# Doubling steps of a blocked RWKV-7 scan on one core: the first two groups issued alternately, the second on the off-diagonal quarters of TensorE's array

## The chip, the cores and the metric

The kernel runs on one core of a Trainium2 chip. The metric is the device time of one execution in microseconds (us), lower is better. The median of three runs before the change is 2687.97 us (2686.44 to 2688.4).

## What is computed

One layer of a diffusion backbone over 512 latent and 128 context tokens of width 1024: input projection, two parallel mixers (a Fourier mixing and a bidirectional RWKV-7 scan), output projection, then an expert-choice FFN with 16 experts. The change touches the scan only. In the reference it is a recurrence over tokens, for 16 heads of 64 channels and both directions:

```python
def wkv7_scan(r, w, k, v, kk, a, s0, reverse):
    def step(S, inp):
        r_t, w_t, k_t, v_t, kk_t, a_t = inp
        sa = jnp.einsum('bhij,bhj->bhi', S, -kk_t)
        S = (S * w_t[:, :, None, :] + sa[..., None] * (kk_t * a_t)[:, :, None, :]
             + v_t[..., None] * k_t[:, :, None, :])
        y = jnp.einsum('bhij,bhj->bhi', S, r_t)
        return S, y
```

## The kernel before, in words

`layer` runs five phases one after the other: `front_phase` (input projection, to about 500 us), `scan_phase` (L434, about 500 to 1316 us), `merge_phase`, `expert_phase` (from about 1600 us, the larger part of the rest) and `combine_phase`. Nothing of a later phase is loaded or computed during the scan.

**The scan.** It makes eight passes (`tiles`, `body(i, m, first, last)`), one for each 128 channels, that is two heads. The tokens lie in five chunks of 128. A chunk, two directions and two heads make four problems, each with a triangular 128x128 system, whose inverse is built by doubling: the diagonal 64x64 quarters are inverted by five rounds on blocks of 64, a sixth round fills in the off-diagonal quarter. A pass has these stages:

- **Pair stage** (`pair_products`, L869 to L893; five chunks in the order `ORDER`). PE forms the products of a chunk: L877 and L878 for the masked matrices, and the 64x64 products into two PSUM banks `b_m(0)`, `b_m(1)` (L886, L888, L892), 20 of them. Row half h of the array, that is partitions `HALVES[h]`, writes bank `b_m(h)`; its outputs go to both column halves. ACT copies them out (L766 to `TD`, L767 to `Mq`, which a trace calls `x`), twice each. POOL then masks: `tt_start` (L647, L649) on `TD` for each chunk, `m_off` (L666) to `Mo`, `t_start` (L654, L658) to `T`. DVE masks `NRR` (L1186). In between, PE, ACT and DVE carry the output norm of the pass before (`norm`).
- **Rounds** (`for rd in range(TOP)`, six). The five chunks are three groups, `GROUPS`: chunks at places 0 and 1, at 2 and 3, and at 4. A group has two PSUM banks, `b_z(b)` and `b_dt(b)`. In a round, for each group: `z_step` makes Z = Mo^T TD (L908; in the sixth round L914) into `b_z`; ACT evicts it to `Z` (L775, `evict`); `t_step` makes T^T Z (L933; sixth round L929) into `b_z` and Z^T T (L939) into `b_dt`; DVE adds the first to `TD` (L1229; in the fifth round L1232, to `TT`), the second to `T` (L1235). POOL writes the next round's `Mo` once the group's `z_step` has read the last (L666). In the sixth round ACT writes `TT` instead (L787). A 64x64 matmul of fp32 is two passes through the array, each with a weight load, and stands as two in the x count. Both halves of the diagonal are used in turn: half 0 (rows and columns 0 to 63) and half 1.
- **Jobs in the rounds.** A round has three places (`PER_ROUND`) in which PE, ACT and DVE carry the next pass's preparation, `front(n, i + 1, 1 - m)`, in this order: J_DEC0, J_DEC1, J_NORM | J_RATE0, J_RATE1, J_VT | J_ST, J_SCAN1, J_SUB1 | J_KEYS1, J_NONE0, J_NONE1 | J_NONE2, J_BONUS. PE's matmul of a job waits until the PSUM of the job before is read (`s_free`). J_DEC0: PE L824, ACT a table load and two sigmoids (L695), a square (L700). J_DEC1: PE L824, ACT L695 again, after which DVE runs the prefix sums (L1086). J_BONUS: DVE L1157. The first pass has no norm, the last pass no jobs of a next pass.
- **Chain** (`part`, `output`): from L967 on, the states chunk by chunk, some 28 us.

**The order of the queues** is written by hand and each engine keeps it. In a round of before:

- PE: z(0), z(1), job 0, t(0) (both products), z(2), job 1, t(1), job 2, t(2). In the sixth round two filler matmuls (`fill(2)`, L945) stand before t(1) and before t(2).
- ACT: evict 0, evict 1, job 0, evict 2, job 1, job 2.
- DVE: for each group in turn: its job, the add to `TD`, the add to `T`.

Of the kernel before, what the change touches and what calls it, by code (L numbers as in the profile page):

```python
# [433 lines left out]
def scan_phase(nc, d, ident, lora, spare):  # L434
# [12 lines left out]
    NG, NPROB = NT, 4  # L447
    ORDER = [0, 3, 1, 2, 4]
    POS = {g: n for n, g in enumerate(ORDER)}
    GROUPS, CHUNKS, BANKS = ((0, 2), (2, 4), (4, 5)), (slice(0, 4, 3), slice(1, 3, 1), slice(4, 5, 1)), ((0, 1), (2, 3), (4, 5))  # L450
    TOP = LEVELS - 1
    steps = [(b, l) for l in range(1, LEVELS) for b in range(len(GROUPS))]
# [17 lines left out]
    with ExitStack() as ctx:  # L470
# [160 lines left out]
        def _(g_):  # L631
# [10 lines left out]
            def body(i, m, first, last):  # L642
# [37 lines left out]
        def _(act):  # L680
# [129 lines left out]
        def _(pe):  # L810
# [57 lines left out]
            def pair_products(i, m, n):  # L868
# [26 lines left out]
            def z_step(i, n):  # L895
                b, l = steps[n]
# [7 lines left out]
                for c, p in enumerate(range(*GROUPS[b])):  # L904
                    if l < TOP:
                        for q in range(NPROB):
                            for hs in HALVES:
                                last = pe.matmul(ps_of(b_z(b), b)[hs, c, q, :], Mo[hs, p, q, :], TD[hs, p, q, :], start=True, stop=True)  # L908
                    else:
                        g = ORDER[p]  # L910
                        for h in range(2):
                            for dr, hs in enumerate(HALVES):
                                os_ = HALVES[1 - dr]
                                last = pe.matmul(ps_of(b_z(b), b, 2)[hs, c, h, :], Mq[os_, g, 2, h, :], TT[os_, g, 2 * dr + h, os_], start=True, stop=True)  # L914
                last.then_inc(s_z, 1)

            def t_step(i, n):
                b, l = steps[n]
                pe.wait_ge(s_zs, i * NS + n + 1)
                if l == 1:  # L920
                    pe.wait_ge(s_ti, i * NGR + b + 1)
                else:
                    pe.wait_ge(s_t, i * ND + n - NGR + 1)
                pe.sem_inc(s_pe_turn, 1)
                for c, p in enumerate(range(*GROUPS[b])):
                    if l == TOP:
                        for h in range(2):
                            for dr, hs in enumerate(HALVES):
                                last = pe.matmul(ps_of(b_z(b), b, 2)[hs, c, h, :], T[hs, p, 2 * dr + h, :], Z[hs, p, h, :], start=True, stop=True)  # L929
                    else:  # L930
                        for q in range(NPROB):
                            for hs in HALVES:
                                last = pe.matmul(ps_of(b_z(b), b)[hs, c, q, :], T[hs, p, q, :], Z[hs, p, q, :], start=True, stop=True)  # L933
                last.then_inc(s_dtt, 1)
                if l < TOP:
                    for c, p in enumerate(range(*GROUPS[b])):
                        for q in range(NPROB):
                            for hs in HALVES:
                                last = pe.matmul(ps_of(b_dt(b), b)[hs, c, q, :], Z[hs, p, q, :], T[hs, p, q, :], start=True, stop=True)  # L939
                    last.then_inc(s_dt, 1)  # L940

            def fill(n):

# [53 lines left out]
            def body(i, m, first, last):  # L997
# [8 lines left out]
                pe.wait_ge(s_ms, i * NG + NG)  # L1006
                if not first:
                    pe.wait_ge(s_gs, i)
                for rd in range(TOP):
# [12 lines left out]
                fill(3)  # L1022
                pe.wait_ge(s_full, i * NGR + NGR)
                part(i, m, CT, "X")
# [38 lines left out]
        def _(v):  # L1063
# [148 lines left out]
            def body(i, m, first, last):  # L1212
# [3 lines left out]
                        norm(n, i - 1, 1 - m)  # L1216
                for dr in range(2):
                    scaled_state(m, dr, 0)
                for rd in range(TOP):
                    for b in range(NGR):  # L1220
                        if not first and PER_ROUND * rd + b in (2, NSLOT):
                            norm(N_BONUS if rd == 0 else N_GATE, i - 1, 1 - m)
                        if not last and PER_ROUND * rd + b < NSLOT:
                            front(PER_ROUND * rd + b, i + 1, 1 - m)
                        n = NGR * rd + b
                        if rd < TOP - 1:
                            v.wait_ge(s_dtt, i * NS + n + 1)
                            if rd < TOP - 2:
                                v.tensor_tensor(wide_of(TD, b), wide_of(TD, b), ps_of(b_z(b), b), ALU.add).then_inc(s_tt, 1)  # L1229
                            else:  # L1230
                                for hs in HALVES:
                                    ins = v.tensor_tensor(TT[hs, CHUNKS[b], :, hs], wide_of(TD, b)[hs], ps_of(b_z(b), b)[hs], ALU.add)  # L1232
                                ins.then_inc(s_tt, 1)
                            v.wait_ge(s_dt, i * ND + n + 1)
                            v.tensor_tensor(wide_of(T, b), wide_of(T, b), ps_of(b_dt(b), b), ALU.add).then_inc(s_t, 1)  # L1235
                for n in CHAIN[:-1]:
                    state(i, m, n)

# [758 lines left out]
```

## Time and profile before

| | |
|---|---|
| median of three runs | 2687.97 us |
| the profiled execution's own time | 2687.13 us |
| its span, first to last instruction | 2685.2 us |
| mean granted TensorE clock | 0.961 of full speed |
| PE, DVE, ACT, POOL busy | 90%, 37%, 23%, 14% of the span |
| one pass of the scan, second to seventh | 102.3 to 102.9 us |
| of it: pair stage, rounds 1 to 5, round 6, chain and rest | 16.7, 50.2, 5.5, 29.8 us |

The profile is of one execution, on one core. PE's busy time counts overlapping matmuls once, and a matmul's end is modelled. A group's busy time adds its instructions without overlap. "Idle before" is the engine's idle time ahead of an instruction and, behind the arrow, what ended it. Times in a timeline count from the span's start.

### The profile page before, as it was taken

How to read it: one execution, taken by the hardware profiler on the slowest of the kernel's cores; microseconds unless marked ns; L12 is line 12 of the kernel's file. 1: busy time of each engine (PE TensorE's matmuls, PEld its weight loads, DVE VectorE, ACT ScalarE, POOL GpSimd, SP SyncE). 2: the span in 40 equal slices, each digit the busy share in tenths (PEclk: the TensorE clock that was granted, in tenths of full speed). 3: DMA queues.
4: the chain of work that ended last, by engine and by line, in shares of the span. 5: the costliest groups of instructions: out<-in, count | busy, mean ns of one | idle time of the engine just before them, and what ended most of it. 6: DMA issues, size and time to landing. Idle time of an engine off the chain costs nothing. (4 is left out here: it accounts for less than half of the span.)

```text
span 2685.2 us, 58051 instructions
## 1 busy us (share of the span) xinstructions
PE 2420.9 (90%) x26165; PEld 1504.4 (56%) x26165; DVE 984.9 (37%) x1737; ACT 615.4 (23%) x1179; POOL 363.8 (14%) x405
## 2 busy tenths in 40 slices
PE   5999996688998998999689949999999999999993
PEld 3999995577787787788445513333333333333331
DVE  3344311658468467475113431121212212121114
ACT  2122222435535445443200100111111111111111
POOL 0000000315315325224000600000000000000000
PEclk8999998799999999999889969999999999999997
DMA  8363331000000000000361179999999999999974
GB/s 339 102 242 103 112 112 60 19 20 5 26 25 5 27 25 5 26 8 5 126 238 43 71 291 401 400 394 392 396 396 395 396 394 382 399 396 395 395 294 162
DMA packets 180715, 538.55 MB, mean 201 GB/s; under 512 B 13254, under 2 KB 53926, under 8 KB 180216
## 3 DMA queue, kind: packets, MB, share of 16 engines
q1 hardware_dynamic: 177400, 524.39, 50.5%
q0 software_dynamic: 3072, 10.49, 1.8%
q8 instruction: 205, 3.36, 0.5%
q14 instruction: 38, 0.31, 0.0%
HBM read 504.15 MB, written 30.70 MB: 199 GB/s over the span
## 5 line engine op out<-in xcount | busy, mean ns | idle before, releaser
L1724 PE MATMUL ps_h_lat<-w_piece,xT 128*64 128x512 f32 x2048 | 456.7, 599 | 8.6 <-DVE hidden L1846 7.5
L1724 PEld LDWEIGHTS ps_h_lat<-w_piece,xT 128*64 128x64 f32 x2048 | 145.7, 138 | 312.9 <-issue 312.9
L1749 PE MATMUL ps_y_lat<-w_piece,hiddenT 128*64 128x512 f32 x1024 | 232.6, 596 | 0.9 <-ACT hiddenT L1610 0.9
L1733 PE MATMUL ps_h_ctx<-w_piece,xT 128*16 128x512 f32 x2048 | 226.1, 593 | 0.0
L1840 DVE TENSOR_TENSOR hidden<-sigmoid_lat,ps_h_lat 64x1024 f32<-64x1024 f32 x32 | 39.1, 1223 | 506.6 <-ACT sigmoid_ctx L1616 506.6
L325 PE MATMUL ps_in<-hT_hi,w_in_hi 128*128 128x320 f32 x752 | 173.3, 312 | 3.0 <-issue 3.0
L666 POOL TENSOR_TENSOR Mo<-x,levels_sb 128x256 f32<-128x256 f32 x200 | 161.9, 832 | 99.2 <-PE ps_scan L908 99.1
L325 PE MATMUL ps_in<-hT_lo,w_in_hi 128*128 128x320 f32 x752 | 172.0, 310 | 0.0
L325 PE MATMUL ps_in<-hT_hi,w_in_lo 128*128 128x320 f32 x752 | 172.0, 310 | 0.0
L908 PE MATMUL ps_scan<-TT_diag,Mo 64*64 64x64 f32 x3200 | 115.0, 220 | 43.8 <-issue 26.6
L1749 PEld LDWEIGHTS ps_y_lat<-w_piece,hiddenT 128*64 128x64 f32 x1024 | 70.2, 137 | 138.3 <-issue 137.7
L1614 ACT ACTIVATE sigmoid_lat<-ps_h_lat 64x1024 f32<-64x1024 f32 x32 | 32.6, 1018 | 469.0 <-PE ps_h_lat L1724 469.0
L1733 PEld LDWEIGHTS ps_h_ctx<-w_piece,xT 128*16 128x16 f32 x2048 | 59.1, 97 | 139.7 <-issue 137.5
L908 PEld LDWEIGHTS ps_scan<-TT_diag,Mo 64*64 64x64 f32 x3200 | 104.9, 135 | 50.8 <-issue 49.4
L325 PEld LDWEIGHTS ps_in<-hT_hi,w_in_hi 128*128 128x128 f32 x752 | 126.2, 189 | 5.3 <-issue 5.1
L325 PEld LDWEIGHTS ps_in<-hT_hi,w_in_lo 128*128 128x128 f32 x752 | 126.4, 189 | 0.0
L325 PEld LDWEIGHTS ps_in<-hT_lo,w_in_hi 128*128 128x128 f32 x752 | 126.1, 188 | 0.0
L933 PE MATMUL ps_scan<-Z,T 64*64 64x64 f32 x3200 | 119.2, 221 | 5.9 <-ACT Z L775 5.3
L1665 POOL DMA_INDIRECT x_scratch<-ye,row_out x16 | 22.8, 1428 | 737.5 <-DVE ye L1853 737.5
L933 PEld LDWEIGHTS ps_scan<-Z,T 64*64 64x64 f32 x3200 | 106.1, 136 | 22.8 <-issue 19.5
L1186 DVE TENSOR_TENSOR NRR<-ps_scan,causal_sb 128x384 f32<-128x384 f32 x160 | 78.0, 548 | 106.2 <-PE ps_scan L878 106.0
L939 PE MATMUL ps_scan<-T,Z 64*64 64x64 f32 x3200 | 116.5, 219 | 0.4 <-issue 0.4
(278 smaller groups left out, 3530.1 us busy)
## 6 DMA issues: line engine op xcount, KB each, us to landing
w_piece<-in_w_e SPq DMA_DIRECT2D x192, 2048.0 KB, 13.5
w_ada<-in_w_ada SPq DMA_DIRECT2D x6, 4096.0 KB, 17.8
w_in_raw<-in_w_in SPq DMA_DIRECT2D x23, 1024.0 KB, 6.3
rkv_scratch<-projected SPq DMA_DIRECT2D x24, 320.0 KB, 6.2
rkv_T<-rkv_scratch SPq DMA_DIRECT2D x8, 960.0 KB, 5.1
gates_scratch<-projected SPq DMA_DIRECT2D x16, 320.0 KB, 6.7
gate_sb<-gates_scratch SPq DMA_DIRECT2D x8, 640.0 KB, 6.3
x<-in_x_sample SPq DMA_DIRECT2D x8, 512.0 KB, 6.5
```

Source lines behind the costliest of these rows:

```text
L325: last = pe.matmul(wide[c % 2][:, b * 512:b * 512 + HALF], w, h[:, k, b * HALF:(b + 1) * HALF], start=(k == 0 and n == 0), stop=(k == KD - ...
L666: ins = g_.tensor_tensor(Mo[:, p, :, :].rearrange("p (e h) n -> p e h n", e=2), Mq[:, ORDER[p], 0:2, :, :], levels[:, l, :, :].unsqueeze(2 ...
L908: last = pe.matmul(ps_of(b_z(b), b)[hs, c, q, :], Mo[hs, p, q, :], TD[hs, p, q, :], start=True, stop=True)
L933: last = pe.matmul(ps_of(b_z(b), b)[hs, c, q, :], T[hs, p, q, :], Z[hs, p, q, :], start=True, stop=True)
L939: last = pe.matmul(ps_of(b_dt(b), b)[hs, c, q, :], Z[hs, p, q, :], T[hs, p, q, :], start=True, stop=True)
L1186: v.tensor_tensor(NRR[:, p, :, :], src[:, 0:3 * P].rearrange("p (a n) -> p a n", a=3), causal[:, dr, :, :], ALU.mult).then_inc(s_am, 1)
L1614: act.activation(sg[UP, :], psA[UP, :], ACT.Sigmoid)
L1665: g_.indirect_dma_start(out=d["x1"], out_offset=bass.IndirectOffsetOnAxis(ap=row[j][:, 0:1], axis=0), in_=ye[j][:, :], in_offset=None, com ...
L1724: last = pe.matmul(psA[rows, cs], x[:, k, A], w[:, q, cs], start=(k == 0), stop=(k == KD - 1))
L1733: last = pe.matmul(psB[GRP[g], :], x[:, k, B], w[:, q, c * 512:(c + 1) * 512], start=(k == 0), stop=(k == KD - 1))
L1749: last = pe.matmul(psY[rows, :], hT[:, f, A], w[:, q, c * 512:(c + 1) * 512], start=(hf == 0 and f == 0), stop=(hf == 1 and f == FK - 1))
L1840: v.tensor_tensor(hid[A, :], sg[UP, :], psA[UP, :], ALU.mult)
```

## The change

- In the pair stage, for the chunks at places 2 and 3 (`CROSSED`, the second group), eight more 64x64 products (16 passes) put T's start on swapped partition halves; ACT copies it to `T` (two more activations of 128x128 for each of the two chunks), ahead of the others, and POOL masks it in place.
- `z_step` and the first product of `t_step` (now `tt_step`) take several groups: for groups 0 and 1 their matmuls are issued alternately, and the second group's read or write the opposite half, so that its `Z` and `T` lie on swapped halves. The semaphores of both groups step together, at the last matmul.
- Z^T T is `dt_step`, for each group by itself; the second group's operands are both on swapped halves, so that it runs on the diagonal.
- The order of the queues. PE: z(0,1), z(2), job 0, tt(0,1), dt(0), job 1, dt(1), tt(2), dt(2), job 2. ACT: evict 0, 1, 2, then jobs 0, 1, 2. DVE: job 0, `TD` adds of groups 0 and 1, `T` add of group 0, job 1, `T` add of group 1, both adds of group 2, job 2. In round 6: PE z(0,1), z(2), J_KT0, tt(0,1), tt(2), without the four fillers.

```diff
@@ POOL, t_start
-                        g_.tensor_tensor(T[:, p, :, :].rearrange("p (e h) n -> p e h n", e=2), Mq[:, ORDER[p], 0:2, :, :],
+                        low = T[:, p, :, :].rearrange("p (e h) n -> p e h n", e=2)
+                        g_.tensor_tensor(low, low if p in CROSSED else Mq[:, ORDER[p], 0:2, :, :],
@@ ACT, body
                     for h in range(2):
+                        if n in CROSSED:
+                            act.activation(T[:, n, h::2, :], b_m(h)[:, 5 * HD:7 * HD].rearrange("p (e n) -> p e n", e=2), ACT.Copy)
...
-                    evict(0)
-                    evict(1)
                     for b in range(NGR):
-                        if b == 1:
-                            evict(2)
+                        evict(b)
+                    for b in range(NGR):
@@ PE, pair_products
+                    if n in CROSSED:
+                        for x, xs in enumerate(HALVES):
+                            for h, hs in enumerate(HALVES):
+                                last = pe.matmul(b_m(h)[HALVES[1 - x], (5 + dr) * HD:(6 + dr) * HD], AR[m][dr][hs, g, 0, xs], B[dr][hs, at(x)],
+                                                 start=True, stop=True)
@@ PE, the steps
+            def problems(bs, l):
+
+                both = [[(b, c, p, q, x) for c, p in enumerate(range(*GROUPS[b])) for q in range(2 if l == TOP else NPROB) for x in range(2)]
+                        for b in bs]
+                return [one for pair in zip(*both) for one in pair]
...
+            def z_step(i, rd, bs):
+                l, n = rd + 1, NGR * rd + bs[-1]
                 if l < TOP:
                     pe.wait_ge(s_mo, i * ND + n + 1)
                 if l == 1:
-                    pe.wait_ge(s_tt0, i * NG + GROUPS[b][1])
+                    pe.wait_ge(s_tt0, i * NG + GROUPS[bs[-1]][1])
...
+                        last = pe.matmul(ps_of(b_z(b), b)[HALVES[x ^ (p in CROSSED)], c, q, :], Mo[HALVES[x], p, q, :], TD[HALVES[x], p, q, :],
+                                         start=True, stop=True)
...
+                last.then_inc(s_z, len(bs))
...
+            def tt_step(i, rd, bs):
...
+                for b, c, p, q, x in problems(bs, l):
+                    hs, ts = HALVES[x], HALVES[x ^ (p in CROSSED)]
...
+                        last = pe.matmul(ps_of(b_z(b), b)[hs, c, q, :], T[ts, p, q, :], Z[ts, p, q, :], start=True, stop=True)
+                last.then_inc(s_dtt, len(bs))
@@ PE, body
                 for rd in range(TOP):
-                    z_step(i, NGR * rd)
-                    z_step(i, NGR * rd + 1)
+                    z_step(i, rd, (0, 1))
+                    z_step(i, rd, (2,))
                     if rd == TOP - 1:
                         turn(J_KT0, i, m, last)
-                    for b in range(NGR):
-                        if b == 1:
-                            z_step(i, NGR * rd + 2)
-                        if not last and PER_ROUND * rd + b < NSLOT:
-                            front(PER_ROUND * rd + b, i + 1, 1 - m)
-                        if rd == TOP - 1 and b:
-                            fill(2)
-                        t_step(i, NGR * rd + b)
+                        slot(PER_ROUND * rd)
+                        tt_step(i, rd, (0, 1))
+                        slot(PER_ROUND * rd + 1)
+                        tt_step(i, rd, (2,))
+                        slot(PER_ROUND * rd + 2)
+                    else:
+                        slot(PER_ROUND * rd)
+                        tt_step(i, rd, (0, 1))
+                        dt_step(0)
+                        slot(PER_ROUND * rd + 1)
+                        dt_step(1)
+                        tt_step(i, rd, (2,))
+                        dt_step(2)
+                        slot(PER_ROUND * rd + 2)
@@ DVE, body
                 for rd in range(TOP):
...
+                    slot(PER_ROUND * rd)
+                    if rd < TOP - 1:
+                        add_tt(rd, 0)
+                        add_tt(rd, 1)
+                        add_t(rd, 0)
+                    slot(PER_ROUND * rd + 1)
+                    if rd < TOP - 1:
+                        add_t(rd, 1)
+                        add_tt(rd, 2)
+                        add_t(rd, 2)
+                    slot(PER_ROUND * rd + 2)
```

## Rows read from the trace of the kernel before

**Rows 1.** Windows, second and seventh pass of eight: stretch, length, busy us (x count), clock, DMA.
```profile
602.48:704.73 102.25, 92.74 (x1868) 80.46 (x1869) 66.68 (x126) 47.03 (x105) 34.61 (x43) 1.00 0.06 19
1114.45:1216.99 102.54, 92.66 (x1868) 80.36 (x1869) 66.70 (x126) 47.04 (x105) 34.65 (x43) 1.00 0.03 7
```

**Rows 2.** Windows of rounds in the second pass, columns as in Rows 1.
```profile
630.79:640.91 10.12, 9.92 (x260) 8.57 (x257) 9.61 (x15) 7.39 (x12) 5.09 (x5) 1.00 0.01 2
...
627.84:669.42 41.58, 36.91 (x1035) 33.33 (x1034) 39.58 (x63) 19.69 (x35) 16.20 (x18) 1.00 0.01 3
```

**Rows 3.** Timeline of PE, second pass: start, length, engine, line, operation [idle before].
```profile
617.69 0.41 PE L892 MATMUL ps_scan<-AR,B 64*64 64x64 f32 x16
619.19 2.08 PE L908 MATMUL ps_scan<-TT_diag,Mo 64*64 64x64 f32 x64 [1.08 <-ACT x L767]
...
625.02 0.68 PE L908 MATMUL ps_scan<-TT_diag,Mo 64*64 64x64 f32 x16 [0.68 <-POOL Mo L666]
626.10 0.49 PE L824 MATMUL ps_scan<-lora,w_dec 64*128 64x128 f32 x4 [0.39 <-ACT sg L695]
...
670.50 0.77 PE L840 MATMUL ps_scan<-ident_sb,K 128*128 128x128 f32 x5
...
674.90 1.55 PE L967 MATMUL ps_scan<-Vt,NRR 128*128 128x64 f32 x12
```

**Rows 4.** Timeline of POOL, second pass, around the start of the doubling rounds.
```profile
616.79 0.92 POOL L647 TENSOR_TENSOR TT_diag<-TT_diag,level_sb 128x256 f32<-128x256 f32 x1 [0.29 <-ACT x L767]
...
624.20 0.67 POOL L666 TENSOR_TENSOR Mo<-x,levels_sb 128x256 f32<-128x256 f32 x1
```

**Rows 5.** Timeline of ACT, second pass.
```profile
618.17 0.28 ACT L766 ACTIVATE TT_diag<-ps_scan 128x128 f32<-128x128 f32 x1 [1.46 <-PE ps_scan L892]
...
618.71 0.35 ACT L767 ACTIVATE x<-ps_scan 128x192 f32<-128x192 f32 x1
...
623.48 1.28 ACT L695 ACT_TABLE_LOAD   x1 [1.58 <-DVE par_cur L1127]
624.78 1.26 ACT L695 ACTIVATE sg<-ps_scan,par_cur 128x512 f32<-128x512 f32 x2
...
626.89 0.36 ACT L775 ACTIVATE Z<-ps_scan 128x256 f32<-128x256 f32 x1
...
673.49 1.36 ACT L787 ACTIVATE x<-ps_scan 64x256 f32<-64x256 f32 x4 [0.50 <-PE ps_scan L929]
```

**Rows 6.** Timeline of DVE, second pass.
```profile
627.84 2.82 DVE L1086 TENSOR_TENSOR_SCAN G_T<-one_sb,sg 128x128 f32<-128x128 f32 x5 [2.76 <-ACTq L697]
...
665.05 1.38 DVE L1232 TENSOR_TENSOR x<-TT_diag,ps_scan 64x512 f32<-64x512 f32 x2
...
667.06 0.82 DVE L1157 TENSOR_TENSOR bonus<-ps_scan,rkv_T 128x640 f32<-128x640 f32 x1
668.01 1.38 DVE L1232 TENSOR_TENSOR x<-TT_diag,ps_scan 64x512 f32<-64x512 f32 x2
...
670.96 0.85 DVE L1232 TENSOR_TENSOR x<-TT_diag,ps_scan 64x256 f32<-64x256 f32 x2
```

**Rows 7.** Timeline of PE, first pass.
```profile
524.03 0.68 PE L908 MATMUL ps_scan<-TT_diag,Mo 64*64 64x64 f32 x16 [0.56 <-POOL Mo L666]
524.64 0.49 PE L824 MATMUL ps_scan<-lora,w_dec 64*128 64x128 f32 x4
```

**Rows 8.** Timeline of PE, last pass, its first round.
```profile
1239.81 0.68 PE L908 MATMUL ps_scan<-TT_diag,Mo 64*64 64x64 f32 x15 [2.08 <-POOL Mo L666]
...
1240.39 1.81 PE L933 MATMUL ps_scan<-Z,T 64*64 64x64 f32 x30
```

**Rows 9.** Windows of the last pass, columns as in Rows 1.
```profile
1240.24:1243.65 3.41, 3.41 (x72) 3.41 (x68) 0.69 (x1) 0.38 (x1) 3.41 (x6) 0.50 0.02 5
1244.68:1266.41 21.73, 21.53 (x724) 21.30 (x722) 11.05 (x20) 4.73 (x9) 9.66 (x15) 1.00 0.02 5
1266.41:1278.74 12.33, 11.83 (x334) 10.19 (x330) 6.79 (x13) 4.67 (x12) 0.00 (x0) 1.00 0.09 31
```

More of the change, by code:

```diff
@@ L449, in scan_phase @@
     POS = {g: n for n, g in enumerate(ORDER)}
+    CROSSED = (2, 3)
     GROUPS, CHUNKS, BANKS = ((0, 2), (2, 4), (4, 5)), (slice(0, 4, 3), slice(1, 3, 1), slice(4, 5, 1)), ((0, 1), (2, 3), (4, 5))
@@ L892, in pair_products @@
                             last = pe.matmul(b_m(h)[xs, (3 + dr) * HD:(4 + dr) * HD], B[dr][hs, at(x)], AR[m][dr][hs, g, 0, xs], start=True, stop=True)
-                last.then_inc(s_m, 1)
-            def z_step(i, n):
-                b, l = steps[n]
+                    if n in CROSSED:
[3 more added lines that the diff above has]
+                                                 start=True, stop=True)
+                last.then_inc(s_m, 1)
+            def problems(bs, l):
[4 more added lines that the diff above has]
+                l, n = rd + 1, NGR * rd + bs[-1]
                 if l < TOP:
@@ L903, in z_step @@
                 pe.sem_inc(s_pe_turn, 1)
-                for c, p in enumerate(range(*GROUPS[b])):
+                for b, c, p, q, x in problems(bs, l):
                     if l < TOP:
-                        for q in range(NPROB):
-                            for hs in HALVES:
-                                last = pe.matmul(ps_of(b_z(b), b)[hs, c, q, :], Mo[hs, p, q, :], TD[hs, p, q, :], start=True, stop=True)
-                    else:
[L910 to L918, printed above, removed]
+                        last = pe.matmul(ps_of(b_z(b), b)[HALVES[x ^ (p in CROSSED)], c, q, :], Mo[HALVES[x], p, q, :], TD[HALVES[x], p, q, :],
+                                         start=True, stop=True)
+                    else:
+                        g, os_ = ORDER[p], HALVES[1 - x]
+                        last = pe.matmul(ps_of(b_z(b), b, 2)[HALVES[x ^ (p in CROSSED)], c, q, :], Mq[os_, g, 2, q, :], TT[os_, g, 2 * x + q, os_],
+                                         start=True, stop=True)
+                last.then_inc(s_z, len(bs))
+            def tt_step(i, rd, bs):
+                l, n = rd + 1, NGR * rd + bs[-1]
                 pe.wait_ge(s_zs, i * NS + n + 1)
                 if l == 1:
-                    pe.wait_ge(s_ti, i * NGR + b + 1)
+                    pe.wait_ge(s_ti, i * NGR + bs[-1] + 1)
                 else:
@@ L924, in t_step, with dt_step @@
                 pe.sem_inc(s_pe_turn, 1)
-                for c, p in enumerate(range(*GROUPS[b])):
[L926 to L940, printed above, removed]
+                for b, c, p, q, x in problems(bs, l):
+                    hs, ts = HALVES[x], HALVES[x ^ (p in CROSSED)]
+                    if l == TOP:
+                        last = pe.matmul(ps_of(b_z(b), b, 2)[hs, c, q, :], T[ts, p, 2 * x + q, :], Z[ts, p, q, :], start=True, stop=True)
+                    else:
+                        last = pe.matmul(ps_of(b_z(b), b)[hs, c, q, :], T[ts, p, q, :], Z[ts, p, q, :], start=True, stop=True)
+                last.then_inc(s_dtt, len(bs))
+            def dt_step(b):
+                for c, p in enumerate(range(*GROUPS[b])):
+                    for q in range(NPROB):
+                        for hs in HALVES:
+                            last = pe.matmul(ps_of(b_dt(b), b)[hs, c, q, :], Z[hs, p, q, :], T[hs, p, q, :], start=True, stop=True)
+                last.then_inc(s_dt, 1)
             def fill(n):
@@ L1008, in body, with slot @@
                     pe.wait_ge(s_gs, i)
+                def slot(n):
+                    if not last and n < NSLOT:
+                        front(n, i + 1, 1 - m)
                 for rd in range(TOP):
-                    z_step(i, NGR * rd)
-                    z_step(i, NGR * rd + 1)
+                    z_step(i, rd, (0, 1))
+                    z_step(i, rd, (2,))
                     if rd == TOP - 1:
                         turn(J_KT0, i, m, last)
-                    for b in range(NGR):
-                        if b == 1:
-                            z_step(i, NGR * rd + 2)
-                        if not last and PER_ROUND * rd + b < NSLOT:
-                            front(PER_ROUND * rd + b, i + 1, 1 - m)
-                        if rd == TOP - 1 and b:
-                            fill(2)
-                        t_step(i, NGR * rd + b)
+                        slot(PER_ROUND * rd)
[3 more added lines that the diff above has]
+                        slot(PER_ROUND * rd + 2)
+                    else:
+                        slot(PER_ROUND * rd)
[6 more added lines that the diff above has]
+                        slot(PER_ROUND * rd + 2)
                 fill(3)
@@ L1218, in body, with slot @@
                     scaled_state(m, dr, 0)
-                for rd in range(TOP):
[L1220 to L1235, printed above, removed]
+                def slot(n):
+                    if not first and n in (2, NSLOT):
+                        norm(N_BONUS if n == 2 else N_GATE, i - 1, 1 - m)
+                    if not last and n < NSLOT:
+                        front(n, i + 1, 1 - m)
@@ new lines, in add_tt @@
+                def add_tt(rd, b):
+                    v.wait_ge(s_dtt, i * NS + NGR * rd + b + 1)
+                    if rd < TOP - 2:
+                        v.tensor_tensor(wide_of(TD, b), wide_of(TD, b), ps_of(b_z(b), b), ALU.add).then_inc(s_tt, 1)
+                    else:
+                        for hs in HALVES:
+                            ins = v.tensor_tensor(TT[hs, CHUNKS[b], :, hs], wide_of(TD, b)[hs], ps_of(b_z(b), b)[hs], ALU.add)
+                        ins.then_inc(s_tt, 1)
@@ new lines, in add_t @@
+                def add_t(rd, b):
+                    v.wait_ge(s_dt, i * ND + NGR * rd + b + 1)
+                    v.tensor_tensor(wide_of(T, b), wide_of(T, b), ps_of(b_dt(b), b), ALU.add).then_inc(s_t, 1)
+                for rd in range(TOP):
+                    slot(PER_ROUND * rd)
[9 more added lines that the diff above has]
+                    slot(PER_ROUND * rd + 2)
```

## The prediction

> **What bounds the kernel now.** The windows of the scan's passes come first: the second and the seventh of eight take 102.25 and 102.54 us, with PE busy for 92.7 [rows 1]. Busy time says PE is the limit. The rounds say otherwise. In round 2 PE is busy for 9.92 of 10.12 us, but DVE for 9.61 too, and from the first prefix sum of round 1 to the end of round 5, 41.58 us, DVE is busy for 39.58 and PE for only 36.91 [rows 2]. So over four fifths of the rounds DVE has 2.0 us of idle time in all. It carries the adds of the doubling and the next pass's preparation, and the change takes nothing from it.
>
> The start of round 1 is bound by another engine. z(2) stands at 625.02, released by POOL's Mo [rows 3], whose last piece ends at 624.87 [rows 4]; POOL itself had last waited at 616.79, for ACT's eviction of the second crossed chunk [rows 4]. Before z(2) PE had already done group 0's t_step, and ACT had started job 0's table load at 623.48 [rows 5].
>
> **What the edits cost, part by part.** All times are for the second pass; passes 3 to 7 repeat it.
>
> *Alternate issue.* 16 passes over the two diagonal quarters last 0.68 us and 64 last 2.08, so 29 ns a pass; 16 passes of L892, which go round all four quarters, last 0.41 [rows 3]. The 15 steps between first and last thus shrink from 0.43 us to 0.16, 11 ns each. I take half of 29, 14.6, each quarter keeping its pace: z(0) with z(1) falls from 1.87 to 0.93, tt(0) with tt(1) likewise; dt stays. That is 1.87 us less PE in each of rounds 1 to 5 and 0.47 in round 6, where four fillers go as well.
>
> Here the Trainium skill speaks against the change. "TensorE: Matmul & The Clock Gate", Part 3, says that weight loads run under in-flight matmuls only where the row group differs, and the new order sends two matmuls in turn to the same row half. L892 alternates the row halves but has both column halves of each in work at once at 11 ns a step, so the trace does not bear the rule out for quarters; by the rule the pair would stay at 1.87.
>
> *Pair stage.* 16 more passes for each crossed chunk, 0.23 us each at 14.6 ns, 0.47 on PE. Two more ACT activations a chunk: four of them run from 618.17 to 619.06, 0.22 apiece, and one alone lasts 0.28 [rows 5], so 0.3 to 0.56; they overlap in a row, I take 0.35. POOL waits for this eviction and then works without a pause to z(2)'s Mo. Its instructions are as many as before. So z(2) can come 0.47 + 0.35 = 0.8 later, at 625.8.
>
> *Round 1, the new order.* z(2) now stands on PE ahead of job 0 and tt(0,1), and on ACT evict 2 ahead of job 0. Behind z(2) thus wait everything of PE, ACT's table load and by that the next pass's preparation. z(2) is out 0.68 after its start, 626.5, evicted in 0.36, so the table load starts at 626.9 instead of 623.48: **+3.4**. With 1.28 for it and 1.26 for the sigmoids, job 1's matmul goes from 626.10 to 629.5 [rows 3, 5]. PE's z(2), job 0, tt(0,1), dt(0) need about 3.4 us (0.47, 1.1 as an estimate from 2048 columns at 2.4 GHz, 0.93, 0.93) and are just done. DVE's prefix sums, before at 627.84 [rows 6], start at 630.95, +3.1, as evict 2 is no longer in their way.
>
> *Rounds 2 to 5.* PE's saving has no taker. DVE's list up to the first add of round 5 (665.05) is the same set in another order. Its 2.0 us of idle time [rows 2] could swallow part of the delay, but it lies before work that hangs on ACT's and PE's jobs, and these hang on the table load. I carry 3.4: the first L1232 goes to 668.45.
>
> *Rounds 5 and 6.* The second L1232 follows at once, where before a T add (0.60) and J_BONUS (0.82) lay between [rows 6]: its end moves from 669.39 to 671.2, +1.8. Round 6's z(0,1) can start there, but z(2) stands on PE before tt(0,1) and waits for T add, J_BONUS, T add and L1232 of group 2, 0.60 + 0.82 + 0.60 + 0.85 = 2.9: to 674.1. Then z(2) 0.23, J_KT0 0.70 of its 0.77 [rows 3], tt(0,1) 0.47 and 0.25 to ACT: 675.75. ACT's L787 took 1.36 for two groups [rows 5]; now three stand behind one another, 2.05: 677.8. The chain's first matmul, before at 674.90 [rows 3], starts at 677.9: **+3.0**. The chain itself is untouched.
>
> *TensorE's clock.* Between the last L892 (617.69, with the new products over at 618.6) and z(2) at 625.8, 7.2 us, PE has 0.93 us of work. In the last pass PE stood idle 2.08 us before 1239.81, the granted clock was 0.50 from 1240.24 to 1243.65 (2.4 to 1.2 GHz), and 30 passes took 1.81 us [rows 8, 9], twice their time. I expect such a fall in every pass. Only z(2) at the low clock: +0.5. All of PE up to job 1 at it: +3.2. Part of the stretch lies in the idle time; I take +1.3.
>
> *First pass.* No norm, so ACT and PE have room in the pair stage; I take POOL, which z(2) waits for there too, as unmoved, and z(2) at 524.03; table load at 525.1, job 1 at 527.75 instead of 524.64 [rows 7], +3.1, the rest as above: +2.7, and 1.3 of clock.
>
> *Last pass.* No jobs, so PE counts. z(2) at 1240.6; then 4.2 us of PE, and the 1.7 that a stretch of 3.41 us at half speed costs, as before, end round 1 at 1246.5 instead of 1244.68: +1.8. Rounds 2 to 4 take 21.73 us, PE busy for 21.53 [rows 9]. New: z(0,1) 0.93, 0.25, two evictions of some 0.57 (0.36 for half as many columns), 0.17, then tt 0.93, dt 0.93 + 0.93, tt and dt of group 2 0.93: 6.2, so 18.6 for three: −3.1. Rounds 5 and 6: 12.33 to 11.7, −0.6. Together −1.9.
>
> **Sum**: 6 × (3.0 + 1.3) + 2.7 + 1.3 − 1.9 = +27.9 on the profiled execution's 2687.13, which lies 0.8 under the median of the runs. Nothing of a later phase overlaps the scan. **2715.**
>
> **Rivals.**
>
> 1. *Absorbed*: DVE's 2.0 us of idle time swallows its part of each delay and the clock falls where PE has room. 6 × 1.0 + 0.7 − 1.9 = +5: 2692. For it: 2.0 us are there. Against: ACT's and PE's jobs are late by the same 3.4. It decides between job 1 of round 1 and round 3. 13%.
> 2. *PE was the bound* (the faster side): DVE's time fills up because PE feeds it late, and from round 2 on each round shrinks by PE's 1.87. A pass: 3.4 + 1.3 − 4 × 1.87 − 0.5 = −3.3; with seven and the last, −25: 2662. For it: 9.92 of 10.12 in round 2. Against: DVE 9.61 there. It decides where DVE's busy share in rounds 2 to 5 falls under some 90%. 11%.
> 3. *The clock falls again*: PE now idles some 2.5 us before z(2) in rounds 4 to 6. Two more stretches of 3.41 us a pass, some 1.3 us each of it on the path: 7 × 2.6 = 18, 2733. 15%.
> 4. *The quarters do not overlap*, the change doesn't do what it says: tt(0,1) +0.93 before job 1, of which ACT's wait hides some, and +0.5 in round 6: 1.5 a pass, and 1.87 in each of the last pass's rounds, 9: 2734. 6%.
>
> **How the numbers follow.** Forecast 55%, at 2715; its own bounds are the clock term (0.5 and 3.2 in seven passes: −6 and +13) and the evictions. Rivals 3 and 4 reach 2734 to 2738, rival 1 stands at 2692. A range of 2690 to 2738 leaves out rival 2 and tails. Measurement tells some 0.2%, 5 us. Slower: 55 + 15 + 6 and 1 of rival 1, 77%. Same: 12% (rival 1). Faster: 11%.
>
> **What the changed profile would show.** Right: z(0,1) of 64 passes in about 1.15 us; in round 1 z(2) near 23.3 us after the pass's start, with job 0 and tt(0,1) behind it; prefix sums near 28.5 after it instead of 25.4; low clock in each pass; DVE still above 90% busy from there to round 5; passes of 106 to 107 us, the last one shorter than 98. Wrong: z(2) released early, or job 1 near 23.6 after the pass's start; rounds 2 to 4 under 8 us with DVE idle; a pass under 102 us.

## The result and the profile after

The changed kernel takes 2753.53 us (median of four runs, 2747.12 to 2760.73) against 2688.18 beside it: ratio 1.0245, 95% interval 1.0219 to 1.0271, so 65 us slower. The forecast was 2715, slower by 28, with a range of 2690 to 2738. The direction was right, the forecast size less than half of the measured one. Pass by pass the first seven are 6.0, 10.7, 10.0, 9.6, 10.6, 11.1 and 5.9 us longer than before, and the last one's chain starts 1.6 us later.

The page of the changed kernel: span, busy time, then PE and its granted clock in 40 slices.

```profile
span 2750.4 us, 58435 instructions
...
PE 2404.2 (87%) x26389; PEld 1486.2 (54%) x26389; DVE 976.6 (36%) x1737; ACT 617.7 (22%) x1211; POOL 356.1 (13%) x405
...
PE   5999995687887878878859958999999999999993
...
PEclk8999997799889988889979969999999999999997
```

The span grew by 65.2 us and PE's busy time fell by 16.7. Of the eleven slices that lay wholly in the scan before (the ninth to the nineteenth) the clock's digit was 9 in all, and is 8 in six now. In the trace TensorE's clock now falls in every pass; before it was at 1.00 from the second to the seventh.

Windows of the second pass (stretch, length, busy us and count of PE, PEld, DVE, ACT, POOL, then clock, DMA): the whole pass; round 1 up to DVE's prefix sums; from there to the first L1249 (the old L1232); from there to the chain; the chain with the pass's rest.

```profile
607.88:720.83 112.95, 91.12 (x1897) 78.81 (x1897) 65.88 (x126) 47.39 (x109) 32.76 (x43) 0.89 0.06 17
626.42:638.49 12.07, 9.47 (x211) 7.51 (x213) 4.22 (x8) 5.47 (x9) 8.61 (x13) 0.58 0.01 3
638.49:676.83 38.34, 27.45 (x959) 24.50 (x955) 34.32 (x57) 19.37 (x35) 12.95 (x15) 0.96 0.01 3
676.83:686.83 10.00, 6.39 (x157) 4.96 (x157) 6.84 (x12) 3.02 (x10) 0.00 (x0) 1.00 0.15 48
686.83:720.83 34.00, 31.71 (x254) 28.66 (x254) 7.42 (x28) 9.09 (x26) 0.00 (x0) 0.85 0.10 32
```

The pass takes 112.95 us instead of 102.25 [rows 1]. The stretch of [rows 2] from the prefix sums on to the end of round 5 answers to the third of these windows and part of the fourth: DVE is busy for 34.3 of 38.3 us, where before it was 35.4 of 37.2. The granted clock is 0.58 in round 1 and 0.85 in the chain. The window before that answers to the third, from the prefix sums to the first L1232:

```profile
627.84:665.05 37.21, 32.55 (x930) 29.63 (x928) 35.42 (x57) 19.31 (x34) 16.20 (x18) 1.00 0.01 3
```

PE's timeline of that pass, the rows that answer to [rows 3] (L919 is the old L908, L940 the old L933, L947 the old L939, L826 the old L824, L923 and L938 the sixth round, L975 the chain's first matmul).

```profile
621.10 0.30 PE L898 MATMUL ps_scan<-B,AR 64*64 64x64 f32 x8
...
626.42 1.96 PE L919 MATMUL ps_scan<-TT_diag,Mo 64*64 64x64 f32 x64 [2.45 <-POOL Mo L668]
630.97 1.12 PE L919 MATMUL ps_scan<-TT_diag,Mo 64*64 64x64 f32 x16 [2.60 <-POOL Mo L668]
632.02 2.08 PE L826 MATMUL ps_scan<-lora,w_dec 64*128 64x512 f32 x4
634.03 1.98 PE L940 MATMUL ps_scan<-Z,T 64*64 64x64 f32 x64
...
637.26 0.49 PE L826 MATMUL ps_scan<-lora,w_dec 64*128 64x128 f32 x4
...
645.09 1.16 PE L940 MATMUL ps_scan<-Z,T 64*64 64x64 f32 x64 [1.44 <-ACT Z L779]
...
682.80 0.45 PE L923 MATMUL ps_scan<-x 64*64 64x64 f32 x8 [1.95 <-DVE x L1249]
...
686.83 1.82 PE L975 MATMUL ps_scan<-Vt,NRR 128*128 128x64 f32 x12 [1.43 <-ACT x L789]
```

z(0,1) waits 2.45 us and z(2) another 2.60, both for POOL's Mo, and z(2) comes at 23.1 us of the pass (630.97 − 607.88), job 0 and tt(0,1) behind it, as forecast (23.3). The low clock sets in at 626.51, with z(0,1), and the lengths show it: z(0,1) 1.96 and tt(0,1) 1.98 us, against 1.16 at full clock in round 2; z(2) 1.12 instead of 0.68, and job 0's matmuls 2.08, where the kernel before has 1.13. The row at 621.10 is one of the added products, four matmuls in 0.30 us.

ACT's timeline of that pass, answering to [rows 5], and DVE's prefix sums, answering to [rows 6].

```profile
632.13 0.38 ACT L779 ACTIVATE Z<-ps_scan 128x256 f32<-128x256 f32 x1 [2.62 <-PE ps_scan L919]
632.53 1.28 ACT L697 ACT_TABLE_LOAD   x1
634.15 1.26 ACT L697 ACTIVATE sg<-ps_scan,par_cur 128x512 f32<-128x512 f32 x2 [0.33 <-PE ps_scan L826]
...
684.64 2.14 ACT L789 ACTIVATE x<-ps_scan 64x256 f32<-64x256 f32 x6 [1.07 <-PE ps_scan L938]
```

```profile
638.49 1.69 DVE L1104 TENSOR_TENSOR_SCAN G_T<-one_sb,sg 128x128 f32<-128x128 f32 x5 [0.42 <-ACTq L699]
...
676.83 2.79 DVE L1249 TENSOR_TENSOR x<-TT_diag,ps_scan 64x512 f32<-64x512 f32 x4
```

The table load starts at 24.65 us of the pass (before: 21.0), the prefix sums at 30.6 (forecast 28.5, before 25.4).

### The profile page after: what moved, and what is told of

The parts are those of the page before. It is cut to its first block and busy times, and to the rows that moved or that the text cites. A ratio compares the mean times of both kernels' runs of the same rounds, so it can differ in the third digit from the quotient of the medians.

```text
span 2750.4 us, 58435 instructions
## 1 busy us (share of the span) xinstructions
PE 2404.2 (87%) x26389; PEld 1486.2 (54%) x26389; DVE 976.6 (36%) x1737; ACT 617.7 (22%) x1211; POOL 356.1 (13%) x405
## 5 line engine op out<-in xcount | busy, mean ns | idle before, releaser
L919 PE MATMUL ps_scan<-TT_diag,Mo 64*64 64x64 f32 x3200 | 88.9, 249 | 78.4 <-POOL Mo L668 41.8
L947 PE MATMUL ps_scan<-T,Z 64*64 64x64 f32 x3200 | 127.4, 233 | 5.3 <-issue 5.3
L919 PEld LDWEIGHTS ps_scan<-TT_diag,Mo 64*64 64x64 f32 x3200 | 79.3, 159 | 85.8 <-issue 85.0
L947 PEld LDWEIGHTS ps_scan<-T,Z 64*64 64x64 f32 x3200 | 117.5, 149 | 8.8 <-issue 6.2
L1790 PE MATMUL ps_y_ctx<-w_piece,hiddenT 128*16 128x256 f32 x2048 | 116.7, 380 | 0.0
```

Source lines behind the costliest of these rows:

```text
L919: last = pe.matmul(ps_of(b_z(b), b)[HALVES[x ^ (p in CROSSED)], c, q, :], Mo[HALVES[x], p, q, :], TD[HALVES[x], p, q, :], start=True, stop ...
L1790: last = pe.matmul(psYB[GRP[g], 0:256], hT[:, f, B], w[:, q, g * 256:(g + 1) * 256], start=(hf == 0 and f == 0), stop=(hf == 1 and f == FK ...
```

## The experiments

The expectation of each experiment stands ahead of its result. Ratios are to the kernel before, beside it on the same chip; its medians are 2687.59 to 2688.18 throughout. "Order" below stands for what waits behind what, "clock" for TensorE's.

### Fillers back in round 6 (e1)

```diff
                         slot(PER_ROUND * rd + 1)
+                        fill(4)
                         tt_step(i, rd, (2,))
```

> The changed kernel with the four fillers of round 6 back (four in a row, before tt(2)). Theory A (the chain's 4 us a pass are the clock, and the removed fillers let it fall): passes 2 to 6 lose up to 4.1 us each in the chain, and the time comes to 2728 to 2738. Rival B (the fall comes from the idle time before round 6's z(2) and before the chain's first matmul, which four fillers of 0.17 us don't close): chain still 34 us, 2750 to 2756. The rounds up to the first L1232 stay as they are by both.

Measured: 2736.05 us, ratio 1.0181 (1.0164 to 1.0198), 17.5 us under the changed kernel. The second pass and its chain:

```profile
608.47:717.48 109.01, 88.46 (x1901) 75.70 (x1901) 65.89 (x126) 47.43 (x109) 34.16 (x43) 0.92 0.06 17
687.66:717.48 29.82, 27.27 (x254) 24.30 (x254) 7.41 (x28) 9.10 (x26) 0.00 (x0) 1.00 0.12 36
```

The chain is back at 29.8 us with the clock at 1.00, in each of the first seven passes, as theory A had it. So the 4 us of the chain are the clock, and four fillers are enough to keep it. They are not the only condition: the changed kernel's first and seventh pass have none and their chain takes 29.8 us too. What decides there was not tried. The rounds of the second pass stay as they were.

### Fillers wherever PE now idles (e2)

```diff
+                fill(8)
                 for rd in range(TOP):
                     z_step(i, rd, (0, 1))
+                    if rd:
+                        pe.wait_ge(s_t, i * ND + NGR * rd - 2)
+                    fill(0 if last and rd > 1 else (18, 0, 3, 10, 8, 9)[rd])
                     z_step(i, rd, (2,))
...
-                fill(3)
+                fill(10)
                 pe.wait_ge(s_full, i * NGR + NGR)
```

> The changed kernel with fillers where PE now idles: 8 before round 1's z(0,1), 18 between it and z(2), 3, 10, 8 and 9 there in rounds 3 to 6, 10 instead of 3 before the chain. Nothing else is moved, so the order's cost stays and the clock's goes. Theory (of the 65 us, the order costs 3 to 4 us a pass, the clock 6): clock 1.00 in passes 2 to 7, the prefix sums 28.5 to 29 us after a pass's start, chain 29.8, passes of 105.5 to 106.5 us, 2710 to 2722. Rival (the order itself costs all of the round-1 delay, the clock only the chain): passes of 108 us, 2730 or more.

Measured: 2715.38 us, ratio 1.0101 (1.0084 to 1.0118), 38 us under the changed kernel without moving a step of it. Windows of the second pass, then PE's round 1:

```profile
608.76:715.00 106.24, 95.13 (x1960) 78.34 (x1960) 65.78 (x126) 47.40 (x109) 34.12 (x43) 0.97 0.06 18
637.06:675.16 38.10, 31.56 (x966) 26.62 (x964) 34.30 (x56) 19.48 (x35) 14.29 (x15) 0.91 0.01 4
675.16:685.17 10.01, 9.41 (x187) 6.66 (x181) 6.84 (x12) 3.02 (x10) 0.00 (x0) 1.00 0.15 48
685.17:715.00 29.83, 27.28 (x254) 24.31 (x254) 7.42 (x28) 9.08 (x26) 0.00 (x0) 1.00 0.12 36
```

```profile
627.30 1.16 PE L919 MATMUL ps_scan<-TT_diag,Mo 64*64 64x64 f32 x64
628.39 3.10 PE L953 MATMUL ps_scan<-causal_sb 128*128 128x384 bf16 x18
631.86 0.68 PE L919 MATMUL ps_scan<-TT_diag,Mo 64*64 64x64 f32 x16 [0.36 <-POOL Mo L668]
...
635.59 0.49 PE L826 MATMUL ps_scan<-lora,w_dec 64*128 64x128 f32 x4
```

The prefix sums start at 28.3 us of the pass, where the forecast had put them for the order alone (25.4 + 3.1 = 28.5), and passes 3 to 5 take 105.9 us. That is +3.6 over before (102.25 [rows 1]), and a low stretch of 3.41 us is left in each, some 46 us after its start, so the order, with the longer pair stage, costs at most that. z(2) is at 23.1 us of the pass, as in the changed kernel. The theory held, its clock of 1.00 not quite.

### Round 1 in the old order (e4), and with fillers (e5)

```diff
 PE, body
                     z_step(i, rd, (0, 1))
-                    z_step(i, rd, (2,))
+                    if rd:
+                        z_step(i, rd, (2,))
...
                         dt_step(0)
+                        if not rd:
+                            z_step(i, rd, (2,))
 ACT, body
-                    for b in range(NGR):
+                    for b in range(NGR if rd else 2):
                         evict(b)
                     for b in range(NGR):
+                        if not rd and b == 1:
+                            evict(2)
```

> The changed kernel with round 1 alone in the old order: z(2) behind dt(0) on PE, evict 2 behind job 0 on ACT. Theory (z(2) waiting for POOL's Mo ahead of job 0 is what delays the pass's preparation by 3.4 us, and leaves PE idle so that the clock falls): prefix sums back at 25.5 to 26.5 us after a pass's start instead of 30.6, z(2) behind tt and dt, passes of 106 to 108.5 us, the chain's clock perhaps still low: 2712 to 2728. Rival (the pair stage's extra work and z(0,1)'s wait for both groups' Mo make the delay): 2740 or more.

> e4_round1 with fillers besides: 8 before round 1's z(0,1), 3, 10, 8 and 9 before z(2) in rounds 3 to 6, 10 before the chain. Theory (what is left of e4's 25 us over the kernel before is mostly the clock): clock 1.00 nearly throughout, chain 29.8 in all passes, passes of 102.8 to 103.5 us, 2688 to 2697. Rival (order and pair stage still cost 3 us a pass): above 2703.

Measured: e4 2712.71 us, ratio 1.0090 (1.0073 to 1.0107); e5, which adds e2's fillers but for the 18 of round 1, 2693.9 us, ratio 1.0021 (1.0011 to 1.0031). PE's round 1 in e4, and e4's second and third pass:

```profile
625.88 1.68 PE L921 MATMUL ps_scan<-TT_diag,Mo 64*64 64x64 f32 x64 [2.45 <-POOL Mo L668]
...
631.49 0.63 PE L921 MATMUL ps_scan<-TT_diag,Mo 64*64 64x64 f32 x16
632.06 0.49 PE L828 MATMUL ps_scan<-lora,w_dec 64*128 64x128 f32 x4
```

```profile
607.33:711.50 104.17, 87.16 (x1896) 74.59 (x1897) 67.28 (x126) 47.37 (x109) 33.15 (x43) 0.93 0.06 18
711.50:818.48 106.98, 88.05 (x1896) 76.26 (x1897) 67.17 (x126) 47.17 (x109) 32.70 (x43) 0.94 0.06 18
```

Both came out in their theory's range. z(2) no longer waits: it comes at 631.49 behind dt(0), and job 1 follows it. From the second pass on the prefix sums start at 25.3 to 26.0 us of the pass, against 25.4 before the change, although the pair stage is as long as in the changed kernel and z(0,1) still waits 2.45 us. So neither the added products nor the joint wait of groups 0 and 1 delays the prefix sums; z(2)'s place does. The two passes differ by 2.8 us: the third has the low clock in its chain, and e5 has no such passes. Taken together, as differences to the kernel before: 65.3 us for the change, 27.8 with fillers, 25.1 with round 1's old order, 5.9 with both. The two causes overlap (37.5 and 40.2 us taken away singly, 59.4 together): with round 1 in the old order the low stretch at its start is 3.41 us long or absent, and no longer 10.24. That z(0,1) waits 2.45 us does not decide it: e4 has this wait in every pass from the second on, and a low stretch behind it in the second, fourth and seventh only.

### Only ACT's queue in the old order (e8)

```diff
-                    for b in range(NGR):
+                    for b in range(NGR if rd else 2):
                         evict(b)
                     for b in range(NGR):
+                        if not rd and b == 1:
+                            evict(2)
```

(The edit is e4's on ACT, with PE as in the changed kernel. It moves evict 2 in round 1 alone, and not in every round, as the expectation says.)

> The changed kernel with ACT alone in the old order (evict 2 behind job 0 in every round); PE still has z(2) ahead of job 0. It divides the round-1 delay between the two queues. Theory: the table load is off the path, but the sigmoids wait for job 0's matmul behind z(2) on PE, so only about 1 us a pass comes back: 2742 to 2752. Rival (ACT's queue holds the delay): prefix sums near 27 us after a pass's start and 2730 or less.

Measured: 2748.28 us, ratio 1.0231 (1.0216 to 1.0246), 5 us under the changed kernel. ACT in the second pass's round 1:

```profile
633.59 1.28 ACT L697 ACT_TABLE_LOAD   x1
638.91 1.27 ACT L697 ACTIVATE sg<-ps_scan,par_cur 128x512 f32<-128x512 f32 x2 [4.04 <-PE ps_scan L828]
```

The table load starts at 21.0 us of the pass again and is done 4.04 us before the sigmoids can start; they wait for job 0's matmul, which stands behind z(2) on PE. They start at 26.3 us of the pass, just where the changed kernel has them (634.15 − 607.88). The delay sits in PE's queue. The time lies in the theory's range, but not for its reason, 1 us a pass: the chain takes 33.8 us and more in four passes here instead of five, which is 4 of the 5 us.

### The quarters taken out (e3, e7)

```diff
-    CROSSED = (2, 3)
+    CROSSED = ()
```

> The changed kernel with CROSSED empty: same order and semaphores, but both groups on the diagonal quarters and no extra products and evictions in the pair stage. z(0,1) and tt(0,1) take 1.9 us instead of 0.95. Theory (DVE and the order bound the rounds, PE's saving has no taker): pair stage and z(2) 0.6 us earlier, tt(0,1) 0.9 later in round 1, the last pass 8 us longer, PE fuller and the clock less low: 2745 to 2765. Rival (PE's saving is worth its 1.87 us a round and hides under the order's cost): 65 us and more longer, above 2790.

> e6_reordered with CROSSED empty: same order, no quarters, no extra work in the pair stage. It prices the quarters where the order does not hide them. Theory (DVE bounds rounds 2 to 5, PE's 1.87 us a round have no taker but in rounds 1 and 6 and in the last pass): 6 to 20 us above e6. Rival (PE is a bound in the rounds again): 40 us or more above e6, 1.87 us in five rounds of seven passes being 65.

Measured: e3 2784.87 us, ratio 1.0341 (1.0311 to 1.0372), 31 us above the changed kernel; e7 2717.54 us, ratio 1.0112 (1.0098 to 1.0127), 28 us above e6. Both lie between the theory and its rival, so neither held. tt(0,1) in rounds 1 and 2 of e3:

```profile
639.31 3.62 PE L940 MATMUL ps_scan<-Z,T 64*64 64x64 f32 x64
...
651.62 2.10 PE L940 MATMUL ps_scan<-Z,T 64*64 64x64 f32 x64 [0.47 <-ACT Z L779]
```

At full clock it lasts 2.10 us there and 1.16 in the changed kernel: the quarters do what they say. Of the 31 us some 8 are the clock, as e3's chain takes 33.9 us in the first and the seventh pass too; up to the chain its passes 2 to 7 are 3.0 to 3.8 us longer. e7 has two passes without a low stretch. The fourth, and its stretch from the prefix sums to the first add of round 5:

```profile
817.88:922.91 105.03, 93.36 (x1881) 81.33 (x1882) 67.50 (x126) 46.98 (x105) 35.20 (x43) 1.00 0.06 18
844.01:882.98 38.97, 31.71 (x924) 29.15 (x922) 35.72 (x56) 19.34 (x34) 16.01 (x17) 1.00 0.01 3
```

The quarters are thus worth 3 to 4 us a pass, not nothing, as the theory had it, nor the 9 us of PE that they save. And without them a pass of e7 takes 105.03 us, where the kernel before takes 102.25 [rows 1] with as many matmuls in its steps, and that stretch 38.97 instead of 37.21. So this order costs some 3 us a pass by itself. That it is the joining of two groups' steps, and not DVE's order or the fillers, is likely but not shown.

### What bounds the rounds of the kernel before (e10, e11)

e10, DVE lighter (the bonus is left out of the output):

```diff
-                else:
-                    v.tensor_tensor(bonus[m][:, :], bonus[m][:, :], K[1][:, :], ALU.add)
...
-                    v.tensor_tensor(y, y, bonus[m][:, :], ALU.add)
```

e11, PE fuller (z(2) three times over in rounds 2 to 5):

```diff
-                        for q in range(NPROB):
+                        for q in [q for _ in range(3 if b == 2 and l > 1 and i < KD - 1 else 1) for q in range(NPROB)]:
```

> The kernel before with two DVE instructions a pass left out of the rounds: the add of the bonus to y in round 1's last job (0.97 us) and the add of the second direction's keys to the bonus in round 4's first (0.83 us); so the bonus is left out of the output. Theory (DVE bounds rounds 2 to 5 of the kernel before): up to 1.8 us in each of six or seven passes, 2676 to 2682. Rival (PE bounds them): nothing, 2686 to 2689.

> The kernel before with z(2)'s matmuls issued three times over (same inputs, same result) in rounds 2 to 5 of the first seven passes: 0.93 us more PE work in a round, 3.7 a pass. Theory (DVE bounds these rounds): most of it hides, 0 to 1.2 us a pass, 2688 to 2696. Rival (PE bounds them, so that the quarters' 1.87 us a round should have come out): 3 us and more a pass, 2709 to 2714.

Measured: e10 2679.05 us, ratio 0.9971 (0.9958 to 0.9983), so 8.9 us less, as the theory had it; e11 2702.22 us, ratio 1.0056 (1.0042 to 1.0070), 14.3 us more, between the theory (up to 2696) and its rival (from 2709). Windows of a pass and of prefix sums to first L1232 (in e11's listing the third pass):

```profile
602.81:703.97 101.16, 92.37 (x1868) 80.25 (x1869) 65.17 (x124) 47.07 (x105) 33.97 (x43) 1.00 0.06 19
628.19:664.29 36.10, 32.18 (x930) 29.42 (x928) 33.88 (x56) 19.32 (x34) 15.51 (x18) 1.00 0.01 3
```

```profile
710.58:815.05 104.47, 96.25 (x1996) 84.09 (x1997) 67.27 (x126) 47.20 (x105) 34.13 (x43) 1.00 0.06 18
735.96:774.48 38.52, 35.13 (x1026) 32.33 (x1024) 35.90 (x58) 19.45 (x34) 15.67 (x18) 1.00 0.02 4
```

Of 1.8 us taken from DVE 1.1 come back in each pass (101.16 instead of 102.25), of 3.7 us given to PE 2.2 appear (104.47). Neither engine alone bounds the rounds: about 60% of what is taken from DVE comes back, and about 60% of what PE is given appears. The natural reading is that they hand the path to each other. It rests on one place for each: e11 lengthens z(2), ahead of job 1 and t(1), and work at another place in PE's queue was not tried.

### A version meant to beat both (e6, e9)

The quarters kept; z(2) behind dt(0) and evict 2 behind job 0 in all rounds; DVE's six adds of round 5 ahead of J_BONUS; round 6 on PE as z(0,1), J_BONUS, tt(0,1), z(2), tt(2), J_KT0; fillers.

```diff
+                fill(8)
                 for rd in range(TOP):
                     z_step(i, rd, (0, 1))
-                    z_step(i, rd, (2,))
                     if rd == TOP - 1:
+                        slot(J_BONUS)
+                        pe.wait_ge(s_t, i * ND + NGR * rd - 2)
+                        fill(0 if last else 6)
+                        tt_step(i, rd, (0, 1))
+                        z_step(i, rd, (2,))
+                        fill(0 if last else 3)
+                        tt_step(i, rd, (2,))
                         turn(J_KT0, i, m, last)
...
 e9 besides, ahead of tt(0,1) in rounds 1 to 5
+                        if rd:
+                            pe.wait_ge(s_t, i * ND + NGR * rd - 2)
+                        fill(0 if last else (1, 9, 16, 6, 6)[rd])
```

> A version meant to be faster: z(2) behind dt(0) and evict 2 behind job 0 in every round; in round 5 DVE makes all six adds before J_BONUS; in round 6 PE runs z(0,1), J_BONUS, tt(0,1), z(2), tt(2), J_KT0; fillers before round 1 and in round 6. Theory (round 6 waits for DVE's list, and J_BONUS and J_KT0 in front of it are in the way): first L1232 to chain 7.2 to 8 us instead of 10.0, the rest as e5: 2670 to 2682, faster than the kernel before. Rival (the wait only moves to L787 on ACT or to the T adds): 9.5 us and more, 2690 or above.

> e6_reordered with fillers also between z(0,1) and tt(0,1) in rounds 1 to 5 (1, 9, 16, 6 and 6), where PE waits for ACT's evictions. Theory (e6's passes of 101.5 and 103.1 us differ by the clock alone): all passes 101.2 to 101.8 us, 2680 to 2686, faster than the kernel before by 0.1 to 0.3%. Rival (fillers get in PE's way and return what the clock gives): 2688 or above.

Measured: e6 2689.98 us, ratio 1.0010 (1.0001 to 1.0018), a miss: passes 2, 4 and 6 have 13.65 us at the low clock and take 103.0 to 103.3 us, the other four of the first seven 101.2 to 102.0. e9 2683.95 us, ratio 0.9987 (0.9978 to 0.9996), 4 us under the kernel before and in the theory's range. Its second pass and the stretch from prefix sums to the first add of round 5:

```profile
601.71:703.58 101.87, 90.70 (x1951) 75.20 (x1952) 67.11 (x126) 47.20 (x109) 32.18 (x43) 1.00 0.06 19
627.01:664.56 37.55, 32.14 (x1012) 26.49 (x1010) 35.62 (x56) 19.39 (x35) 14.63 (x19) 1.00 0.01 4
```

The pass is at 101.87 and the stretch at 37.55 us, against 102.25 and 37.21 before: with four quarters in use, round 1 in order and the clock held, rounds 2 to 5 of this pass are not shorter at all (over passes 2 to 7 the stretch takes 36.9 to 37.5 us). The quarters give back what this order costs without them (e7), and little more. What e9 gains is in round 6, 9.3 instead of 9.85 us from the first add of round 5 to the chain, and in the last pass. The expected 7.2 to 8 us did not come. DVE's two adds to T, ACT's evictions of Z, then PE's J_BONUS, fillers and tt(0,1) in e9's round 6:

```profile
667.39 1.28 DVE L1263 TENSOR_TENSOR T<-T,ps_scan 128x512 f32<-128x512 f32 x2
```

```profile
668.30 0.66 ACT L779 ACTIVATE Z<-ps_scan 128x256 f32<-128x256 f32 x2 [3.64 <-PE ps_scan L925]
```

```profile
668.16 1.35 PE L848 MATMUL ps_scan<-bonus,headones_sb 128*128 128x512 f32 x4
669.35 1.14 PE L955 MATMUL ps_scan<-causal_sb 128*128 128x384 bf16 x6
670.41 0.69 PE L940 MATMUL ps_scan<-Z,T 64*64 64x64 f32 x32
```

The adds to T are over at 668.67 and the evictions at 668.96, but tt(0,1) starts at 670.41, since PE, which reached J_BONUS at 668.16, still has it and then the six fillers to run. The order of round 6 and its fillers took back some 1.4 us of what they were to bring in this pass.

## Why the prediction was right and wrong

**Right: what waits in round 1.** "Behind z(2) thus wait everything of PE, ACT's table load and by that the next pass's preparation." z(2) came at 23.1 us of the pass (forecast 23.3) and the table load 3.6 us later than before (3.4). e4 removed this by moving z(2) and its eviction, and e8, which moves the eviction alone, showed that PE's queue holds it. The quarters overlap: 64 passes in 1.16 us, where 1.15 was said, against 2.10 in e3. The rule of the Trainium skill, "TensorE: Matmul & The Clock Gate", Part 3, that a weight load runs under a matmul in flight only where their row groups differ, is not borne out for two quarters of one row half by these two lengths.

**Right: most of the order's cost.** The forecast without its clock term was +3.0 us for a pass of the middle; e2 shows +3.6 with a little low clock left. The absence of a gain in rounds 2 to 5 was right too (38.34 us against 37.21, and 37.55 in e9). Its reason was not: "PE's saving has no taker" rested on DVE alone. The saving is worth 3 to 4 us a pass (e3, e7), and the order with joined steps costs some 3, for which the sum has no term in rounds 2 to 5; the two cancel. e11 shows PE to share the path.

**Wrong: "The chain itself is untouched."** Its instructions are the same, but it took 33.9 to 34.2 us in passes 2 to 6 instead of 29.8, because the granted clock is 0.5 in a stretch of 10.24 us that begins 1.1 us after its start. The prediction had the four removed fillers and the wait before round 6's z(2) in it, and its sum priced both at nothing for the chain's clock. They cost 5 × 4.1 = 21 us. e1 put four fillers back, and the chain was 29.8 in every pass.

**Wrong: the size of the clock term.** "Part of the stretch lies in the idle time; I take +1.3." Measured by e2 against the changed kernel, the prefix sums lose 2.3 us a pass and rounds 2 to 5 0.2, 7 × 2.5 = 17 us with the first pass counted like the others, where 9 were forecast (7 × 1.3), inside the prediction's own bounds of 0.5 and 3.2 a pass. A low stretch in round 1 is not one of 3.41 us, as the last pass had shown it, but 10.24, and most of PE between z(2) and job 1 runs in it. So passes of 112 to 113 us stand where 106 to 107 were said, which is what they take in e2. In all the clock was 38 of the 65 us, as far as e2's fillers give it back; the forecast had 9. Order 7 × 3.6 = 25, clock 17 and 21, last pass 1.6: together 65. Rival 3, two more stretches a pass, named this and priced it at 18 us on top, too little: the second pass has one more stretch in its rounds, where it costs little (38.34 us against 38.10 in e2), and one in the chain, which hides none of it.

**Wrong, smaller: the last pass.** Forecast was −1.9 us. Measured is +1.6: its round 2 begins 29.9 us after the pass's start instead of 27.7, rounds 2 to 4 take 20.9 us instead of 21.8 (forecast 18.6, 6.2 a round where it is 7.0), and rounds 5 and 6 together 12.6 instead of 12.3 (forecast 11.7). The term that was mis-sized is the round: z and tt at half their length take 0.3 us out of one, not 1.0. In its round 2 tt(0,1) comes 2.4 us after z(0,1), as the forecast had it (2.5); what is longer is behind it, where PE stands still for 0.57 us within group 2's product, for a reason that the profile does not show.

**Wrong, of little effect.** The 30 passes in 1.81 us at the low clock are not "twice their time": in the kernel before 32 take 1.15 at full clock, so the factor is some 1.7. Job 0's "1.1 as an estimate from 2048 columns at 2.4 GHz" does not follow, as these make 0.85; its matmuls last 1.13 in the kernel before.

## What to carry to other kernels

Before a step is put ahead of others in an engine's queue, look at what releases it and add up everything behind it on every engine; here 8 small matmuls that wait for GpSimd's mask, put ahead of the rest, cost 40 of the 65 us (e4), more than halving the time of others in the same queue gave. Where TensorE is made faster inside a path that other engines share, its idle time grows, and the price of a lower clock can be paid later, in whatever is dense behind it, as here in the chain; so price the stage behind the change at the low clock too, and look for fillers that the change removes. A new order has a price even where every step is the same: here it was about what the quarters gave (e7), and it belongs in the sum.

## What the runs showed of the hardware

64x64 products spread over all four quarters of the array, each with its own weight load, run at 1.8 times the pace of those in the two diagonal ones: 64 passes in 1.16 us against 2.10, also when two matmuls in turn use the same row half and both row halves write one PSUM bank. The number of weight loads and matmuls is the same in both.

TensorE's clock fell at 626.51, in round 1, after PE had stood idle for 2.45 us, and again at 687.95, in the chain, after waits of 1.95 and 1.43 us. Both low stretches lasted 10.24 us, although PE was busy for 7.6 and 9.7 us of them:

```profile
626.51:636.75 10.24, 7.64 (x167) 5.86 (x168) 2.83 (x6) 4.84 (x7) 8.52 (x13) 0.50 0.01 2
687.95:698.19 10.24, 9.71 (x45) 9.29 (x45) 0.74 (x3) 2.43 (x8) 0.00 (x0) 0.50 0.31 99
```

In the kernel before, the one low stretch of the rounds from the second pass on was 3.41 us [rows 9]. The same idle time does not always bring the fall (e4), and what makes a stretch 10.24 us long was not tried.
